# Moving the down weights' requests from SyncE's queue to ScalarE's, in a hybrid S5 / attention encoder with a mixture of experts

## The chip, the core and the metric

The kernel runs on one core of a Trainium2 chip. The metric is device time of that core in microseconds (us). Weights come from device memory (HBM) into SBUF by the core's 16 DMA engines. A transfer is asked for by an instruction on the queue of an engine: SyncE (SP), ScalarE (ACT) or GpSimd (POOL). The trace shows such an instruction as SPq, ACTq or POOLq and the transfers that follow as packets of queue q1 (asked for by SyncE), q10 (by ScalarE) and q0 (by GpSimd).

## The reference

Two layers over 256 tokens of width 1024 in float32. Layer 0 mixes tokens with a bidirectional S5 scan, layer 1 with neighbourhood attention. After each comes a mixture of 32 experts of which each token uses two, then a gated input embedding ("ple"). The part that matters here:

```python
for g in range(N_GROUPS):                       # 4 groups of 8 experts
    a = jnp.einsum('td,edf->tef', t, w_gate[g]) # 1024 -> 256
    u = jnp.einsum('td,edf->tef', t, w_up[g])   # 1024 -> 256
    act = jax.nn.silu(a) * u * combine[:, g, :, None]
    y = y + jnp.einsum('tef,efd->td', act, w_down[g])   # 256 -> 1024
```

Each expert has three weight matrices of 1 MB: gate, up and down. All 32 experts of both layers are loaded, 96 MB a layer.

## The kernel before

The tokens are sorted by expert (gather, line 1765) and the experts are worked through in 16 pairs a layer. For pair p TensorE does `gate_up(p)` (line 1794, 32 matmuls), then, one pair behind, the transposes of the activations of pair p-1 (line 1806), two pairs behind the combination `combine(p-2)` (line 1835), and `down(p-1)` (line 1825, 16 matmuls). So the program of TensorE is gate_up(p), act_T(p-1), combine(p-2), down(p-1), gate_up(p+1), and so on. ScalarE does `silu(p)` (line 847) when gate_up(p) is done, and `out_hi(p-1)` (line 855), two evictions of the outputs of down(p-1), the second when down(p-1) is done (semaphore `d_done`). VectorE takes those further (line 1317).

The weights lie in six ring slots, one for each expert, so for three pairs at a time. A slot has a part for gate and up, and a part for down, and each part is asked for again when its last reader is done. The first three pairs of a layer are asked for in full before the layer's experts begin. After that SyncE's program is: gate and up of pair p once gate_up(p-3) is done (four transfers of 1 MB, `load_gate_up`, lines 437 and 438), then the downs of pair p-1 once down(p-4) is done (two transfers of 1 MB, `load_down`, line 446), then pair p+1. At the end of a layer stand the two downs of pair 14 and the two of pair 15. Then come the weights of the ple stage (line 426). PE waits for gate and up of a pair on one semaphore of the slot (`loaded`), for down on another (`down_loaded`).

Of the kernel before, what the change touches and what calls it, by code (L numbers as in the profile page):

```python
# [48 lines left out]
NP = NE // 2  # L49
# [13 lines left out]
def program(nc, I, out):  # L63
    ctx = ExitStack()
    with ctx:
        sems = {}

        def S(name):
            if name not in sems:
                sems[name] = ctx.enter_context(nc.semaphore(name))  # L70
            return sems[name]
# [4 lines left out]
        def at(name, shape, dtype, off):  # L76
            return nc.alloc_sbuf_tensor_at(name, shape, dtype, offset=off)
# [70 lines left out]
        ring = [at(f"ring{s}", [P, RS], F32, A_R + s * RS * 4) for s in range(4)]  # L148
# [10 lines left out]
        items = []  # L159
# [9 lines left out]
        moe_item = []  # L169
# [26 lines left out]
        prev, nth, last, cnt = [], [], {}, {}  # L196
        for n, (s, _) in enumerate(items):
            prev.append(last.get(s))
            last[s] = n
            cnt[s] = cnt.get(s, 0) + 1  # L200
            nth.append(cnt[s])
# [4 lines left out]
        done = {IT["w_in"]: ("u_done", 1)}  # L206
# [9 lines left out]
        down_loaded = [S(f"down_loaded{s}") for s in range(6)]  # L216
# [160 lines left out]
        def overflow(eng, i, body, first=None, last=None):  # L377


            eng.wait_ge(S("many_ready"), i + 1)  # L380
            with eng.If(eng.value_load(many[0:1, 0:1], min_val=0, max_val=2 * T) > 0):
                if first:
                    first()
                with eng.Fori(0, NOV) as n:
                    body(n)
                if last:
                    last()
# [24 lines left out]
        def _(sp):  # L412
            def load(n):
                s, parts = items[n]
                if prev[n] is not None:
                    name, value = done[prev[n]]
                    sp.wait_ge(S(name), value)
                for j, (c, src) in enumerate(parts):
                    w = 1
                    for m in src.shape[1:]:  # L420
                        w *= m
                    dst = ring[s][:, c:c + w]
                    if len(src.shape) == 3:
                        dst = dst.rearrange("p (k n) -> p k n", k=src.shape[1])

                    sp.dma_start(dst, src).then_inc(loaded[s], 48 - 16 * (len(parts) - 1) if j == 0 else 16)

            def load_gate_up(n, first):

                s, (gate_, up_, down_) = items[n]  # L430
                if not first:
                    i, e = (0, n - moe_item[0]) if n < moe_item[1] else (1, n - moe_item[1])
                    sp.wait_ge(S("gu_done"), NP * i + e // 2 - 2)
                elif prev[n] is not None:
                    name, value = done[prev[n]]
                    sp.wait_ge(S(name), value)
                sp.dma_start(ring[s][:, 0:2048], gate_[1]).then_inc(loaded[s], 32)
                sp.dma_start(ring[s][:, 2048:4096], up_[1]).then_inc(loaded[s], 16)

            def load_down(n, first):  # L440

                s, (gate_, up_, down_) = items[n]
                if not first:
                    name, value = done[prev[n]]
                    sp.wait_ge(S(name), value)
                sp.dma_start(ring[s][:, 4096:6144], down_[1]).then_inc(down_loaded[s], 16)

            sp.dma_start(lam[:, 0], I["s5_lam_re"][0].rearrange("d g p -> g d p")).then_inc(S("lam_loaded"), 16)
# [34 lines left out]
            for i in range(2):  # L483
                m0 = moe_item[i]
                for e in range(6):
                    if items[m0 + e][0] == 4:
                        if i == 0:
                            sp.wait_ge(S("x_ready"), 1)
                        else:
                            sp.wait_ge(S("pv_done"), NH)  # L490
                    load_gate_up(m0 + e, True)
                    load_down(m0 + e, True)
                for p in range(3, NP + 1):
                    if p < NP:
                        load_gate_up(m0 + 2 * p, False)
                        load_gate_up(m0 + 2 * p + 1, False)
                    if p >= 4:
                        load_down(m0 + 2 * p - 2, False)
                        load_down(m0 + 2 * p - 1, False)
                wviews = [I["moe_w_gate"][i].rearrange("g j (p k) n -> p (g j) (k n)", k=KD),  # L500
                          I["moe_w_up"][i].rearrange("g j (p k) n -> p (g j) (k n)", k=KD),
                          I["moe_w_down"][i].rearrange("g j (p k) n -> p (g j) (k n)", k=2)]

                def more(n):
                    sp.wait_ge(S(f"ov_free{i}"), n + 1)
                    e = n % NE
                    for c, w in enumerate(wviews):
                        sp.dma_start(ring[S_OV][:, 2048 * c:2048 * c + 2048],
                                     w[:, bass.ds(e, 1), :].rearrange("p e n -> p (e n)"))\
                            .then_inc(S(f"ov_loaded{i}"), 16)  # L510

                for n in (IT["ple"][i][1], IT["ple"][i][0], IT["ple"][i][2]):
                    load(n)
                if i == 0:
                    load(IT["qkv"][0])
                sp.wait_ge(S("d_done"), 2 * NP * (i + 1))
                overflow(sp, i, more, lambda: sp.sem_inc(S(f"ov_free{i}"), 1),
                         lambda: sp.wait_ge(S(f"ov_free{i}"), NOV + 1))
                if i == 0:
                    for n in IT["qkv"][1:] + IT["wo"]:  # L520
                        load(n)
# [170 lines left out]
        def _(ac):  # L692
# [117 lines left out]
            def square(i, t):  # L810
                ac.wait_ge(x_part[i], 2 * t + 2)
                ac.activation(hsq[:, t, :], x[:, t, :], ACT.Square, accum_out=fss[:, t:t + 1]).then_inc(S("fss_ready"), 1)

            def x_evict(i, t):
                ac.wait_ge(S("x_T"), 2 * (TT * i + t) + 1)
                ac.activation(hT[:, 0:4, P * t:P * t + P], PS[:, 2 * t, :].rearrange("p (k t) -> p k t", k=4),
                              ACT.Copy).then_inc(S("xT_a"), 1)

            def token_split(i, t):

                ac.wait_ge(S("frstd_ready"), TT * i + t + 1)
                link(ac.activation(hf[:, t], x[:, t, :].rearrange("p (a k) -> p k a", k=KD), ACT.Copy,
                                   scale=frstd[:, t:t + 1]))
                ac.activation(hhi[:, t], hf[:, t], ACT.Copy).then_inc(S("hhi_ready"), 1)
# [13 lines left out]
            def gather_evict(i, k):  # L838
                ac.wait_ge(S("gather_done"), KD * i + k + 1)
                ac.activation(xg[:, k, :], PS[:, GBANK[k], :], ACT.Copy, scale=gT[:, i, k:k + 1])\  # L840
                    .then_inc(S("xg_ready"), 1)
# [8 lines left out]
            def out_hi(i, p):  # L850
                for n in range(2):
                    ac.wait_ge(S("d_done"), 2 * (NP * i + p) + n + 1)
                    if n == 0 and NP * i + p:
                        ac.wait_ge(S("comb_done"), NP * i + p)
                    ac.activation(ohi[:, 512 * n:512 * n + 512], PS[:, 2 + n, :], ACT.Copy)\  # L855
                        .then_inc(S("ohi_ready"), 1)

            def moe(i):
                square(i, 1)
                x_evict(i, 1)  # L860
                token_split(i, 1)
                ac.wait_ge(S("top_ready"), i + 1)
                for t in range(TT):
                    ac.activation(gex[:, t, :], lg[:, t, NE:NE + NG], ACT.Exp, bias=ngm[:, t:t + 1],
                                  accum_out=gsum[:, t:t + 1])
                ac.activation(e21[:, :], dlt[:, :], ACT.Exp).then_inc(S("gex_ready"), 1)
                ac.wait_ge(S("gT_loaded"), 80)
                for k in range(KD):
                    gather_evict(i, k)
                for p in range(NP):  # L870
                    silu(i, p)
                    if p:
                        out_hi(i, p - 1)
                out_hi(i, NP - 1)
                ac.wait_ge(S("p_T"), i + 1)
                ac.activation(pT[:, :, :].rearrange("p k t -> p (k t)"), PS[:, 0, :], ACT.Copy).then_inc(S("pT_ready"), 1)
                moe_more(i)
# [1160 lines left out]
```

## Time and profile before

| | us |
|---|---|
| median of 3 runs | 876.13 |
| lowest to highest | 876.1 to 878.23 |
| the profiled execution | 876.75 |
| its span in the trace | 875.0 |
| PE busy | 776.4 (89%) |
| ACT busy | 237.9 (27%) |
| data moved | 245.46 MB |

The span is the time from the first to the last instruction in the trace; the execution's own time is 1.75 us more. Where a page has 40 slices, each is 21.9 us. The experts of layer 0 run from 183 to 403 us, those of layer 1 from 623 to 843 us.

### The profile page before, as it was taken

Reading aid. Unit: us, or ns where it says so; the run is one execution under the profiler, and the core shown is the slowest. Engines: PE = TensorE matmul, PEld = TensorE weight load, DVE = VectorE, ACT = ScalarE, POOL = GpSimd, SP = SyncE. Lnnn points to the kernel's source line nnn. Section 1 sums busy time; section 2 is a strip of 40 time slices with the busy share of each in tenths; the row PEclk is TensorE's granted clock in tenths of the full one; section 3 lists DMA queues with packets and bytes.
Section 4 is the critical chain, followed back from the end, with each engine's and each line's share of the span. In section 5 each row is a group of like instructions: output and inputs, shape, how many; then the busy total and the mean of one; then the engine's idle time right before and its main releaser. Section 6 shows DMA issues by size and latency. Waiting matters only on the chain.

```text
span 875.0 us, 10464 instructions
## 1 busy us (share of the span) xinstructions
PE 776.4 (89%) x3995; PEld 425.9 (49%) x3995; DVE 395.4 (45%) x720; ACT 237.9 (27%) x422; POOL 191.0 (22%) x198
## 2 busy tenths in 40 slices
PE   2667879599999998999999878996999999998997
PEld 1556734543433333346878654545533343333456
DVE  6996742623232322136668658515322232222264
ACT  3323123331111101016575444422310111100153
POOL 5874500221110110000056364002211011010000
PEclk9988979699999999999999959996999999999999
DMA  6035070979999999996787660175199999999761
GB/s 217 1 56 194 5 289 1 390 281 425 421 421 420 421 421 419 422 411 218 260 209 248 250 194 1 54 300 223 57 422 421 420 421 422 421 420 421 321 253 48
DMA packets 61091, 245.46 MB, mean 281 GB/s; under 512 B 19667, under 2 KB 20721, under 8 KB 36081
## 3 DMA queue, kind: packets, MB, share of 16 engines
q1 hardware_dynamic: 56752, 240.36, 69.1%
q0 software_dynamic: 1600, 4.26, 2.1%
q8 instruction: 33, 0.54, 0.3%
q10 hardware_dynamic: 2688, 0.17, 0.2%
q14 instruction: 18, 0.14, 0.0%
HBM read 243.16 MB, written 1.60 MB: 280 GB/s over the span
## 4 chain that ended last, share of the span: by engine, by line
PE 83%; DVE 7%; issue 5%; ACT 2%; POOL 2%; DMA 1%; SPq 0%; ACTq 0%; DVEq 0%; POOLq 0%
PE PS L1794 26%; PE PS L1825 13%; PE PS L1545 10%; PE PS L1835 7%; PE PS L1727 3%; PE PS L2008 3%; PE PS L1765 2%; PE PS L1669 2%; PE PS L1967 2%; PE PS L1988 2%; PE PS L1603 2%; PE PS L1915 2%; PE PS L1806 1%; PE PS L1684 1%; POOL qrs L685 1%
## 5 line engine op out<-in xcount | busy, mean ns | idle before, releaser
L1794 PE MATMUL PS<-ring,xe 128*64 128x512 f32 x1024 | 231.0, 604 | 15.9 <-issue 13.5
L1794 PEld LDWEIGHTS PS<-ring,xe 128*64 128x64 f32 x1024 | 79.8, 139 | 163.7 <-issue 163.7
L1825 PE MATMUL PS<-ring,actT 128*64 128x512 f32 x512 | 116.9, 598 | 1.7 <-DVE actT L1303 1.4
L612 POOL COPY xe<-xg 128x512 f32 x60 | 47.1, 786 | 300.1 <-PE PS L1794 297.7
L1317 DVE TENSOR_TENSOR olo<-PS,ohi 128x512 fp32r<-128x512 f32 x64 | 44.3, 692 | 123.5 <-ACT ohi L855 123.5
L1303 DVE COPY actT<-PS 128x256 f32<-128x256 f32 x32 | 13.6, 425 | 175.6 <-PE PS L1806 175.6
L855 ACT ACTIVATE ohi<-PS 128x512 fp32r<-128x512 f32 x64 | 38.3, 598 | 153.0 <-PE PS L1825 153.0
L1008 DVE SCALAR_TENSOR_TENSOR ringr<-ring,gT,dwh 128x512 fp32r<-128x512 f32 x80 | 62.9, 838 | 26.7 <-ACT dwh L726 25.4
L847 ACT ACTIVATE act<-PS 128x256 f32<-128x256 f32 x32 | 12.3, 385 | 225.5 <-PE PS L1794 225.5
L1825 PEld LDWEIGHTS PS<-ring,actT 128*64 128x64 f32 x512 | 34.7, 136 | 67.1 <-issue 67.1
L1545 PE MATMUL PS<-ringr,rawh 128*128 128x512 f32 x160 | 63.4, 396 | 0.8 <-DVE ringr L1008 0.8
L1545 PE MATMUL PS<-dwh,rawh 128*128 128x512 f32 x160 | 62.3, 389 | 0.0
L1545 PE MATMUL PS<-dwh,rawl 128*128 128x512 f32 x160 | 62.3, 389 | 0.0
L726 ACT ACTIVATE dwh<-ring,gT 128x512 fp32r<-128x512 f32 x80 | 52.7, 719 | 34.4 <-PE PS L1545 29.8
L1835 PE MATMUL PS<-ohi,selT 128*128 128x512 f32 x128 | 53.4, 418 | 0.3
L1835 PE MATMUL PS<-olo,selT 128*128 128x512 f32 x128 | 50.2, 392 | 0.0
L1727 PE MATMUL PS<-ring,yT 128*128 128x512 f32 x64 | 32.1, 659 | 5.1 <-DVE yT L1173 5.1
L1545 PEld LDWEIGHTS PS<-ringr,rawh 128*128 128x128 f32 x160 | 30.0, 188 | 7.9 <-issue 1.9
L579 POOL TENSOR_TENSOR rstd<-ms,mhalf 128x2 f32<-128x2 f32 x4 | 2.9, 718 | 140.4 <-DVE ms L990 137.1
L1545 PEld LDWEIGHTS PS<-dwh,rawl 128*128 128x128 f32 x160 | 30.1, 188 | 6.5 <-issue 0.5
L1545 PEld LDWEIGHTS PS<-dwh,rawh 128*128 128x128 f32 x160 | 30.0, 188 | 6.4
L2008 PE MATMUL PS<-ring,oT 128*128 128x512 f32 x64 | 27.9, 594 | 0.5 <-DVE oT L1489 0.5
(323 smaller groups left out, 1031.3 us busy)
## 6 DMA issues: line engine op xcount, KB each, us to landing
ring<-in_moe_w_gate SPq DMA_DIRECT2D x64, 1024.0 KB
ring<-in_moe_w_up SPq DMA_DIRECT2D x64, 1024.0 KB
ring<-in_moe_w_down SPq DMA_DIRECT2D x64, 1024.0 KB, 24.2
ring<-in_nat_w_qkv SPq DMA_DIRECT2D x6, 2048.0 KB
ring<-in_ple_w_gate SPq DMA_DIRECT2D x4, 2048.0 KB
ring<-in_s_w_out SPq DMA_DIRECT2D x2, 2048.0 KB
ring<-in_nat_w_o SPq DMA_DIRECT2D x2, 2048.0 KB
ring<-in_s_w_in SPq DMA_DIRECT2D x1, 2048.0 KB
```

The source lines that it names most:

```text
L612: pool.tensor_copy(xe[:, e % 4, :, :], xg[:, :, bass.ds(first, CAP)]).then_inc(S("xe_ready"), 1)
L726: ins = ac.activation(dwh[:, c, k], dense_w(n, c)[0][:, k], ACT.Copy, scale=gT[:, g, 2 * c + k:2 * c + k + 1])
L855: ac.activation(ohi[:, 512 * n:512 * n + 512], PS[:, 2 + n, :], ACT.Copy)\
L1008: ins = stt(lo[:, k], w[:, k], gT[:, g, 2 * c + k:2 * c + k + 1], dwh[:, c, k].bitcast(F32), ALU.mult, ALU.subtract)
L1317: tt(olo[:, cs], PS[:, 2 + n, :], ohi[:, cs].bitcast(F32), ALU.subtract)\
L1545: ins = mm(PS[:, b0 + t, :], a_[:, 2 * c + k, r], b_, start=(c, k, w) == (0, 0, 0), stop=(c, k, w) == (3, 1, 2))
L1603: ins = mm(PS[:, 4 + a // 2, T * (a % 2):T * (a % 2) + T], w_in[:, k, P * a:P * a + P], s5hT[:, k, :], start=k == 0, stop=k == KD - 1)
L1727: ins = mm(PS[:, 4 + 2 * (n % 2) + w, :], yT[4][:, k, P * t:P * t + P], wv[:, k, 512 * c:512 * c + 512], start=k == 0, stop=k == 3)
L1794: ins = mm(PS[CAP * h_:CAP * h_ + CAP, 0, :].rearrange("p (u f) -> p u f", u=2), xe[:, (2 * p + h_) % 4, k, :], wv[h_][:, k], start=k == 0 ...
L1825: ins = mm(PS[CAP * h_:CAP * h_ + CAP, 2 + n, :], actT[:, k, CAP * h_:CAP * h_ + CAP], wd[h_][:, k, 512 * n:512 * n + 512], start=k == 0, ...
L1835: ins = mm(PS[:, 4 + 2 * n + t, :], selT[:, p % 2, P * t:P * t + P], o_half[:, 512 * n:512 * n + 512], start=(p, w) == (0, 0), stop=(p, w) ...
L2008: ins = mm(PS[:, 6 + n % 2, :], oT[:, k, P * t:P * t + P], wv[:, k, :], start=k == 0, stop=k == KD - 1)
```

## The change

The downs of pairs 3 to 15 of each layer, 52 transfers of 1 MB in all, are asked for by ScalarE instead of SyncE. ScalarE asks for those of pair p+2 behind silu(p) and out_hi(p-1), with the same wait as before (down(p-1) done), which out_hi(p-1) has already had. Gate and up of all pairs, and the downs of pairs 0 to 2, stay with SyncE. Semaphores, buffers and everything else are as before.

```diff
-                for p in range(3, NP + 1):
-                    if p < NP:
-                        load_gate_up(m0 + 2 * p, False)
-                        load_gate_up(m0 + 2 * p + 1, False)
-                    if p >= 4:
-                        load_down(m0 + 2 * p - 2, False)
-                        load_down(m0 + 2 * p - 1, False)
+                for p in range(3, NP):
+                    load_gate_up(m0 + 2 * p, False)
+                    load_gate_up(m0 + 2 * p + 1, False)
...
+            def load_down(n):
+
+                s, (gate_, up_, down_) = items[n]
+                name, value = done[prev[n]]
+                ac.wait_ge(S(name), value)
+                ac.dma_start(ring[s][:, 4096:6144], down_[1]).then_inc(down_loaded[s], 16)
...
                     silu(i, p)
                     if p:
                         out_hi(i, p - 1)
+                        if p + 2 < NP:
+                            load_down(moe_item[i] + 2 * p + 4)
+                            load_down(moe_item[i] + 2 * p + 5)
```

SyncE's program in layer 0, from gate and up of pair 3 on (ring_96 to ring_101 are the six slots), before:

```order
42 L437 DMA ring_98<-in_moe_w_gate 128x2048
43 L438 DMA ring_98<-in_moe_w_up 128x2048
44 L437 DMA ring_99<-in_moe_w_gate 128x2048
45 L438 DMA ring_99<-in_moe_w_up 128x2048
46 L437 DMA ring_96<-in_moe_w_gate 128x2048
47 L438 DMA ring_96<-in_moe_w_up 128x2048
48 L437 DMA ring_97<-in_moe_w_gate 128x2048
49 L438 DMA ring_97<-in_moe_w_up 128x2048
50 L446 DMA ring_98<-in_moe_w_down 128x2048
51 L446 DMA ring_99<-in_moe_w_down 128x2048
52 L437 DMA ring_100<-in_moe_w_gate 128x2048
53 L438 DMA ring_100<-in_moe_w_up 128x2048
```

The same place with the change:

```order
46 L437 DMA ring_96<-in_moe_w_gate 128x2048
47 L438 DMA ring_96<-in_moe_w_up 128x2048
48 L437 DMA ring_97<-in_moe_w_gate 128x2048
49 L438 DMA ring_97<-in_moe_w_up 128x2048
50 L437 DMA ring_100<-in_moe_w_gate 128x2048
51 L438 DMA ring_100<-in_moe_w_up 128x2048
```

The two downs between gate and up of pair 4 and of pair 5 are gone from here, and so at every later pair. ScalarE's program at the beginning of the experts of layer 0 (xg is the gathered input, act the activation, ohi the output's eviction), before:

```order
46 L840 ACTIVATE xg<-PS,gT 128x512 x8
47 L847 ACT_TABLE_LOAD
48 L847 ACTIVATE act<-PS 128x256 x2
49 L855 ACTIVATE ohi<-PS 128x512 x2
50 L847 ACTIVATE act<-PS 128x256
51 L855 ACTIVATE ohi<-PS 128x512 x2
```

The same place with the change:

```order
48 L840 ACTIVATE act<-PS 128x256 x2
49 L848 ACTIVATE ohi<-PS 128x512 x2
50 L856 DMA ring_98<-in_moe_w_down 128x2048
51 L856 DMA ring_99<-in_moe_w_down 128x2048
52 L840 ACTIVATE act<-PS 128x256
53 L848 ACTIVATE ohi<-PS 128x512 x2
54 L856 DMA ring_96<-in_moe_w_down 128x2048
55 L856 DMA ring_97<-in_moe_w_down 128x2048
```

Two requests now stand between each pair of evictions and the next silu.

## Rows read from the trace of the kernel before

**Rows 1.** The page's slices of 21.9 us: DMA share in tenths, and GB/s
```profile
DMA  6035070979999999996787660175199999999761
GB/s 217 1 56 194 5 289 1 390 281 425 421 421 420 421 421 419 422 411 218 260 209 248 250 194 1 54 300 223 57 422 421 420 421 422 421 420 421 321 253 48
```

**Rows 2.** Chain that ended last, layer 0: start us, us, what
```profile
291.98 6.87 PE PS L1794 x32
...
301.07 3.58 PE PS L1825 x16
304.65 6.87 PE PS L1794 x32
...
317.33 1.02 issue
318.34 7.09 PE PS L1794 x32
...
331.23 2.04 issue
333.27 7.09 PE PS L1794 x32
...
361.06 2.02 issue
363.08 8.78 PE PS L1794 x32
...
377.67 0.32 issue
377.99 7.09 PE PS L1794 x32
...
393.62 3.65 PE PS L1825 x16
```

**Rows 3.** The same chain, layer 1
```profile
744.21 6.87 PE PS L1794 x32
...
756.88 1.17 issue
758.04 7.09 PE PS L1794 x32
...
817.95 7.09 PE PS L1794 x32
```

**Rows 4.** DMA, 190.5 to 387.5 us: mean, packets and MB by queue, requests
```profile
DMA packets 11302, 82.42 MB, mean 418 GB/s; under 512 B 1248, under 2 KB 1248, under 8 KB 1248
...
q1 hardware_dynamic: 11292, 82.29, 100.7%
...
ring<-in_moe_w_gate SPq DMA_DIRECT2D x26, 1024.0 KB
ring<-in_moe_w_up SPq DMA_DIRECT2D x26, 1024.0 KB
ring<-in_moe_w_down SPq DMA_DIRECT2D x26, 1024.0 KB, 26.1
```

**Rows 5.** DMA, 240 to 380 us
```profile
DMA packets 8086, 58.93 MB, mean 421 GB/s; under 512 B 898, under 2 KB 898, under 8 KB 898
```

**Rows 6.** Timeline of SyncE's queue: start us, us, line, request
```profile
190.31 0.35 SPq L437 DMA_DIRECT2D ring<-in_moe_w_gate  x1
...
203.30 0.80 SPq L446 DMA_DIRECT2D ring<-in_moe_w_down  x2
...
292.02 7.24 SPq L446 DMA_DIRECT2D ring<-in_moe_w_down  x2
...
350.43 12.84 SPq L446 DMA_DIRECT2D ring<-in_moe_w_down  x4
377.71 0.33 SPq L426 DMA_DIRECT2D ring<-in_ple_w_proj  x1
```

**Rows 7.** DMA, 450 to 460 us: requests of GpSimd (q0) and SyncE (q1) together
```profile
q0 software_dynamic: 470, 1.29, 63.8%
q1 hardware_dynamic: 474, 0.97, 41.6%
```

**Rows 8.** Timeline of ScalarE, 435 us, first request of ScalarE in the program
```profile
435.62 0.58 ACTq L928 DMA_DIRECT2D qkw<-in_nat_q_norm  x1
```

**Rows 9.** DMA, 435.6 to 437.6 us: packets, requests with us to landing
```profile
DMA packets 400, 0.82 MB, mean 410 GB/s; under 512 B 0, under 2 KB 0, under 8 KB 400
...
q1 hardware_dynamic: 400, 0.82, 105.0%
...
qkw<-in_nat_q_norm ACTq DMA_DIRECT2D x2, 0.2 KB, 4.1
```

**Rows 10.** Timeline of ScalarE, one pair of layer 0
```profile
292.03 0.60 ACT L855 ACTIVATE ohi<-PS 128x512 fp32r<-128x512 f32 x1 [1.12 <-PE PS L1825]
298.89 0.38 ACT L847 ACTIVATE act<-PS 128x256 f32<-128x256 f32 x1 [6.27 <-PE PS L1794]
```

**Rows 11.** Line 446 in full: ns min/median/max, and us to landing
```profile
L446 SPq DMA_DIRECT2D ring<-in_moe_w_down x64: 327/481/6296, 113.6 to 801.2; - x64
...
DMA to landing us min/median/max: 8.8/24.2/30.0
```

**Rows 12.** Stretches within gate_up(14): us, busy by engine, granted clock, DMA, GB/s
```profile
363.10:367.40 4.30, 4.30 (x13) 1.57 (x15) 0.11 (x1) 0.00 (x0) 0.00 (x0) 0.60 1.01 419
367.40:371.90 4.50, 4.50 (x23) 1.64 (x20) 0.00 (x0) 0.00 (x0) 0.00 (x0) 1.00 1.02 422
```

More of the change, by code:

```diff
@@ L438, in load_gate_up @@
                 sp.dma_start(ring[s][:, 2048:4096], up_[1]).then_inc(loaded[s], 16)
-            def load_down(n, first):
+            def load_down(n):
                 s, (gate_, up_, down_) = items[n]
-                if not first:
-                    name, value = done[prev[n]]
-                    sp.wait_ge(S(name), value)
                 sp.dma_start(ring[s][:, 4096:6144], down_[1]).then_inc(down_loaded[s], 16)
@@ L491, in _ @@
                     load_gate_up(m0 + e, True)
-                    load_down(m0 + e, True)
-                for p in range(3, NP + 1):
-                    if p < NP:
-                        load_gate_up(m0 + 2 * p, False)
-                        load_gate_up(m0 + 2 * p + 1, False)
-                    if p >= 4:
-                        load_down(m0 + 2 * p - 2, False)
-                        load_down(m0 + 2 * p - 1, False)
+                    load_down(m0 + e)
+                for p in range(3, NP):
+                    load_gate_up(m0 + 2 * p, False)
+                    load_gate_up(m0 + 2 * p + 1, False)
                 wviews = [I["moe_w_gate"][i].rearrange("g j (p k) n -> p (g j) (k n)", k=KD),
@@ L856, in out_hi, with load_down @@
                         .then_inc(S("ohi_ready"), 1)
+            def load_down(n):
+                s, (gate_, up_, down_) = items[n]
+                name, value = done[prev[n]]
+                ac.wait_ge(S(name), value)
+                ac.dma_start(ring[s][:, 4096:6144], down_[1]).then_inc(down_loaded[s], 16)
             def moe(i):
```

## The prediction, made before the changed kernel ran

> **What bounds the kernel now.** I began with the slices of the page [rows 1]. In both stretches of experts the DMA share is 9 tenths or more and the rate stands at 419 to 425 GB/s, slice after slice but the last of each: the weights are loaded at a rate that doesn't rise. Next I read the chain that ended last, in order of time [rows 2]. Up to pair 10 one gate_up follows the other without a wait: 304.65 - 291.98 = 12.67 us for a pair. From pair 11 on (318.34) there is a wait of 1 to 2 us ahead of gate_up ("issue": TensorE waits for nothing that the profile names, which here is a landing), and the period is 333.27 - 318.34 = 14.93 us. That is what six transfers of 1 MB take: 6 x 1.0486 MB / 421 GB/s [rows 5] = 14.94 us, or 2.49 us each. So the experts start with three pairs in store, lose 2.26 us of that lead with each pair, and are bound by DMA from pair 11 to pair 15. Layer 1 repeats it, with the first wait at 758.04 instead [rows 3].
>
> The last gate and up of layer 0 let gate_up(15) begin at 377.99. The position of a transfer in the line tells when it lands. Line: gate and up of pairs 3 to 15 are 13 x 4 = 52 transfers, the downs of the same pairs 26, 78 in all (26 of each kind in [rows 4]). The first is asked for at 190.31 [rows 6], and the queue never runs dry until the last (mean 418 GB/s over the whole stretch, 421 once under way). SyncE's program puts the four downs of pairs 14 and 15 at the end (the row with x4 in [rows 6]), so the last "up" is number 74. 190.31 + 74 x 2.49 = 374.6, and gate_up(15) starts 3.4 us later; the same working for pair 11 (number 50: 314.8) gives 3.5 us against 318.34. I take 3.4 us as start-up and landing. Number 78 is served at 384.5, while the last down starts only at 393.62 [rows 2]. Downs therefore have time to spare at the end, and gate and up have none. **What decides this change is whether gate and up keep their places in the line.**
>
> **The change, part by part.**
>
> *SyncE loses 26 requests a layer.* It spends up to 7.24 us on two of them and 12.84 us on the last four [rows 6], against 0.80 us at the beginning: when some ten transfers are outstanding, a request has to wait for a place. Being rid of that is worth nothing by itself, since the DMA engines are busy all the same [rows 5], and a request accepted earlier is not served earlier at the same rate. The ple weights at 377.71 wait for down(13), not for the queue. Gain 0.
>
> *ScalarE gains 26 requests a layer.* The semaphore wait costs nothing, out_hi has had it. The issue costs about 0.8 us for two (at 203.30 in [rows 6]). They go into the idle time between the second eviction and the next silu, 6.27 us [rows 10]. If ScalarE's requests must wait for a place as SyncE's do, 7.24 us for two would delay silu by 1 us. Silu(p+1) is wanted by gate_up(p+2), which comes after transposes, combine and down, 12.67 - 6.87 = 5.8 us after gate_up(p+1) ends; silu and VectorE's product take about 1 us of them. So cost 0 up to roughly 6.27 + 4.8 = 11 us of blocking, and from there one for one.
>
> *The downs are asked for at the same point of the work*, 0.6 us later (the second eviction). Nothing comes of it alone: they land a median 24.2 us after the request [rows 11].
>
> *The downs are in a line of their own.* This is the term that counts. Where requests of two engines are pending together, the trace has one long stretch: 450 to 460 us, GpSimd's bias loads (q0) beside SyncE's (q1). In it q0 moved 470 packets and q1 474 [rows 7]: the DMA engines take turns, packet for packet. Both kinds of MoE transfer are 1 MB in rows of the same size, so turns by packet, or by request, are equal shares of the rate while both lines have work. The Trainium skill ("DMA: Bandwidth & Descriptors", section Queues, rings and completion order) says that each DMA engine goes round the queues it has work for, packet by packet; the trace agrees (470 to 474), and by the rule the sum is the one below.
>
> With equal shares the two downs of a pair need at most 4 x 2.49 = 9.95 us from request to last byte, instead of 24.2. There is a request of two every 12.7 to 15 us, so the downs are always served soon, and whatever backlog there is falls on gate and up alone. At the end: the last downs (pair 15) are asked for once down(12) is done, a wait of about 2 us and a period of 14.93 before gate_up(15) starts, so some 16.5 us before; less the 3.4 of landing and the 0.6 of ScalarE 12.5 us remain, and they need 9.95. So all 26 downs are served before the last "up", which goes from number 74 to number 78: 4 x 2.49 = +9.95 us, gate_up(15) at 387.9. A second way: a gate_up now has up to four more downs ahead of it. Pair 7 has number 20 + 6 and would get 30, 190.3 + 74.7 + 3.4 = 268.4; without a wait it would start at 291.98 - 2 x 12.67 = 266.64. So the waits start at pair 7 rather than 11, and 268.4 + 8 x 14.93 = 387.8. The two agree.
>
> Nothing behind gate_up(15) gives it back: act_T, combine, down(14) and down(15) follow in a row as they do now, the ple weights wait on down(13) and down(15), and these have moved by the same 9.95 us. The first pairs of layer 1 are asked for after the attention stage, as before. Layer 1 has the same line and the same waits. **Sum: 2 x 9.95 = +19.9 us.** On the profiled execution (span 875.0, time 876.75) that is a span of 894.9; on the median, 876.13, it is 896.0.
>
> *The clock.* After a 2.02 us wait gate_up(14) took 8.78 us in place of 7.09, with a granted clock of 0.60 in its first half and 1.00 in the second [rows 2, 12]. While DMA is the bound this hides in the next wait. If it falls on gate_up(15), where it doesn't now, it costs 1.7 us a layer: 0 to +3.4, I take 0 (of five gate_ups behind a wait in layer 0 one shows it).
>
> **The rivals.**
>
> 1. *One common line, in order of arrival, with contended places.* For: at 435.62 ScalarE asks for a few bytes [rows 8] while one request of SyncE is in work. In the next 2 us the DMA engines move 400 packets of q1 and not one of q10, and it lands after 4.1 us [rows 9]. So ScalarE's request wasn't slipped in among q1's packets as GpSimd's were; making the descriptors may be common to both queues. Against: it had a single request in front of it, so it can't tell a common line from turns by whole requests, and the latter gives the shares above. In a common line with some ten places both engines wait for one, and the downs overtake one or two of the four transfers of gate and up that SyncE still holds: the last "up" goes to number 75 or 76, +2.5 to +5.0 us a layer, 881.1 to 886.1. Chance 0.20.
>
> 2. *Same order as now, no difference.* The common line without overtaking: 876.1, within 2.6. The Trainium skill (same page, section Issuing engines are not separate DMA queues) says that requests from several engines end on the same 16 DMA engines and save only sequencer time, "usually small relative to the DMA itself"; read as "no effect" it gives 876.1. [Rows 5] agree that there is no rate to gain. Chance 0.12.
>
> 3. *Faster, by gate and up going first.* If ScalarE's line got much less than its share, gate and up would run ahead and the downs come last. Number 78 lands at 384.5 + 3.4 = 387.9, the last down now starts at 393.62, so at most 5.7 us a layer, 864.7. It decides if the downs are still in time for each pair; against it is the equal count of [rows 7]. Chance 0.07.
>
> 4. *ScalarE held up beyond its 11 us.* Four requests cost SyncE 12.84 us [rows 6]. If two did that to ScalarE in the nine pairs bound by DMA, 1.8 us each, part of it in TensorE's wait: up to 2 x 9 x 1.8 = 32 us on top, above 900. Against: its line holds at most four or so requests. Chance 0.05.
>
> **How the numbers follow.** Equal shares has 0.56, with its range 893 to 899.4 (with the clock's 3.4 above and a few us below, if the last down isn't quite finished before the last "up"). A measurement of this kernel can tell about 0.3%, 2.6 us. Slower by more than that: 0.56 + 0.05 + most of rival 1 (0.17) = 0.78. Within: 0.12 + 0.03 = 0.15. Faster: 0.07. The range 876 to 900 holds the first case, rival 1 and half of rival 2.
>
> **What would show it.** In the changed trace: the first "issue" of 1 us or more ahead of a gate_up near 268 us (pair 7) rather than 317 (pair 11), and gate_up(15) near 388 in layer 0 and near 817.95 + 19.9 = 837.9 in layer 1; downs landing about 10 us after an ACTq request rather than 24; SyncE's requests for gate and up at about 0.4 us each throughout, as fewer are outstanding; 421 GB/s as before. A common line would show ScalarE's requests at 2 us or more each and landings over 20 us. The forecast is wrong if gate_up(15) of layer 0 begins before 384.

## The result, and the profile of the changed kernel

| | us |
|---|---|
| before, median of 4 runs | 876.12 |
| changed, median of 4 runs (894.98 to 899.08) | 897.79 |
| ratio | 1.0237, 95% interval 1.0208 to 1.0266 |
| changed, the profiled execution | 897.75, span 896.0 |

The change makes the kernel 2.4% slower. The forecast was 896.0, slower with a chance of 0.78.

On the page of the changed kernel, the slices (21.9 us before, 22.4 us now) answer to [rows 1]. The rate in the stretches of experts is the same, 418 to 423 GB/s in the slices that lie wholly in them, and there is a queue q10 of 54.70 MB, nearly all of it the 52 downs:

```profile
DMA  6044061979999999965787650373499999999361
GB/s 212 1 72 172 6 282 45 424 285 418 423 420 421 421 422 421 421 253 189 262 204 263 257 149 1 114 315 135 163 420 421 421 422 421 421 421 421 128 248 47
...
q1 hardware_dynamic: 49264, 185.83, 52.8%
q10 hardware_dynamic: 10176, 54.70, 14.8%
```

The chain that ended last in layer 0 (start us, us, what), which answers to [rows 2]; TensorE's gate_up is line 1797 now:

```profile
266.23 2.56 issue
268.79 7.09 PE PS L1797 x32
...
281.68 1.98 issue
283.66 8.79 PE PS L1797 x32
...
387.63 0.24 issue
387.87 7.09 PE PS L1797 x32
```

The wait ahead of gate_up begins at pair 7 (268.79) where it began at pair 11 (318.34), and gate_up(15) starts at 387.87 instead of 377.99. From gate_up(0), 182.88 us here and 183.25 before, it is 205.0 us instead of 194.7. The same chain in layer 1, which answers to [rows 3]:

```profile
835.21 2.04 issue
837.25 8.78 PE PS L1797 x32
```

Here gate_up(15) comes at 837.25 instead of 817.95, and its first half falls into the lower clock: 8.78 us for 7.09, with a granted clock of 0.61 in its first 4.4 us and 1.00 behind.

The DMA view from 240 to 380 us answers to [rows 5]: mean rate 421 GB/s as before, now from two queues. The second fence is the request's own line (count, ns min/median/max) and its landing, which answers to [rows 11]:

```profile
DMA packets 8099, 58.95 MB, mean 421 GB/s; under 512 B 909, under 2 KB 909, under 8 KB 909
...
q1 hardware_dynamic: 5290, 38.50, 66.1%
q10 hardware_dynamic: 2800, 20.33, 35.0%
```

```profile
L856 ACTq DMA_DIRECT2D ring<-in_moe_w_down x52: 334/413/1192, 202.9 to 820.7; - x52
...
DMA to landing us min/median/max: 8.9/12.0/15.2
```

A down lands 12.0 us after its request in place of 24.2. That is the whole "gain" of the change, and nobody waited for it. Within 4 us in which both lines have work (270 to 274), the DMA view shows who was served:

```profile
q10 hardware_dynamic: 108, 0.88, 53.0%
q1 hardware_dynamic: 112, 0.79, 47.9%
```

108 packets to 112: turns packet for packet. Over the 10 us from 269.5 on it is 275 to 290, and 2.08 to 2.11 MB. This is cleaner evidence than [rows 7]. In the stretch of [rows 7] 156 of the 944 packets are under 512 B. SyncE's 0.97 MB are just 474 rows of 2 KB, so the tiny ones are GpSimd's, and its 470 are about 314 rows of data and 156 tiny packets. The 470 to 474 is a turn each only if a tiny packet counts as a turn.

The DMA view of the end of layer 0, 384.3 to 387 us, shows who was served last:

```profile
q1 hardware_dynamic: 108, 0.75, 66.7%
q10 hardware_dynamic: 14, 0.02, 2.4%
```

ScalarE's last two downs are all but through at 384.3, SyncE's gates and ups run on, almost alone, to 387, and gate_up(15) starts at 387.87. All 26 downs were served ahead of the last "up".

### The profile page after: what moved, and what is told of

It reads as the page before. It is cut to its first block, busy times and chain, and to the rows that moved or that the text cites. A ratio compares the mean times of both kernels' runs of the same rounds, so it can differ in the third digit from the quotient of the medians.

```text
span 896.0 us, 10464 instructions
## 1 busy us (share of the span) xinstructions
PE 782.7 (87%) x3995; PEld 430.4 (48%) x3995; DVE 395.3 (44%) x720; ACT 237.9 (27%) x422; POOL 191.2 (21%) x198
## 3 DMA queue, kind: packets, MB, share of 16 engines
q10 hardware_dynamic: 10176, 54.70, 14.8%
## 4 chain that ended last, share of the span: by engine, by line
PE 82%; DVE 7%; issue 6%; ACT 2%; POOL 2%; DMA 1%; SPq 0%; ACTq 0%; DVEq 0%; POOLq 0%
PE PS L1797 26%; PE PS L1828 13%; PE PS L1548 10%; PE PS L1838 6%; PE PS L2011 3%; PE PS L1730 3%; PE PS L1768 2%; PE PS L1672 2%; PE PS L1970 2%; PE PS L1991 2%; PE PS L1606 2%; PE PS L1918 2%; PE PS L1687 1%; PE PS L1809 1%; POOL qrs L678 1%
## 5 line engine op out<-in xcount | busy, mean ns | idle before, releaser
L1797 PE MATMUL PS<-ring,xe 128*64 128x512 f32 x1024 | 236.5, 616 | 30.6 <-issue 28.3
L1797 PEld LDWEIGHTS PS<-ring,xe 128*64 128x64 f32 x1024 | 84.3, 141 | 180.8 <-issue 180.8
```

Of the source, the lines that this page charges most:

```text
L1797: ins = mm(PS[CAP * h_:CAP * h_ + CAP, 0, :].rearrange("p (u f) -> p u f", u=2), xe[:, (2 * p + h_) % 4, k, :], wv[h_][:, k], start=k == 0 ...
```

## The experiments

The theory: the DMA engines work through a line of 78 transfers of 2.49 us a layer; the two queues take equal turns; a pair can start when the transfers ahead of its last "up" are served, and the change lets downs that nobody needs yet pass gates and ups that TensorE waits for. The rivals: a second queue, or ScalarE's time for its requests, costs by itself; each moved request costs its part; or the loss has one common source outside the layers. Each ratio below is against runs of the kernel before that were taken beside the experiment (medians 876.24 to 876.83 us).

**e8_last_four: only the last downs moved.** ScalarE asks for the downs of pairs 14 and 15 (eight of 52 transfers); the others stay in SyncE's program where they were.

```diff
-                        if p + 2 < NP:
+                        if NP - 4 <= p < NP - 2:
...
+                    if 4 <= p < NP - 1:
+                        for n in (m0 + 2 * p - 2, m0 + 2 * p - 1):
+                            ...
+                            load_down(n)
```

> One part of the change alone: only the downs of pairs 14 and 15 (eight of the 52 transfers) are asked for by ScalarE, those of pairs 3 to 13 by SyncE in the order of the kernel before. Theory (what counts is that these four a layer overtake the last gates and ups): the last up is number 78 as in the full change, gate_up(15) some 205 us behind gate_up(0) instead of 194.8, and the time is that of the full change, 895 to 898, though only eight requests are moved and the waits begin no earlier than pair 12 or 13. Rival (each request moved costs its part): 8/52 of 21.7 us, 879.6.

Measured: 897.49 us (ratio 1.0233, 1.0208 to 1.0258), the time of the full change. The waits ahead of gate_up(11) to (13) are those of the kernel before (1.1 and twice 2.0 us); the large one is ahead of gate_up(14):

```profile
361.42 8.17 issue
369.60 8.40 PE PS L1803 x32
...
383.80 2.56 issue
386.36 8.55 PE PS L1803 x32
```

Gate_up(14) is 187.9 us behind gate_up(0) (181.71) where it was 179.8, so between three and four places were lost at once. Gate_up(15) is 204.7 us behind, as in the full change (205.0). Eight requests do the damage of 52. This run strikes out "each request costs its part" and "ScalarE's time for requests": 44 requests fewer on ScalarE changed nothing.

**e9_not_last: all but the last downs moved.** The downs of pairs 3 to 13 from ScalarE, the last four of each layer from SyncE, behind everything.

```diff
-                        if p + 2 < NP:
+                        if p < NP - 4:
...
+                    if p >= NP - 1:
+                        for n in (m0 + 2 * p - 2, m0 + 2 * p - 1):
+                            ...
+                            load_down(n)
```

> The other part alone: the downs of pairs 3 to 13 (44 transfers) are asked for by ScalarE, those of pairs 14 and 15 by SyncE behind all gates and ups, as in the kernel before. Theory, in the form that the run with ups on ScalarE taught (each pair has its own place in the line, and the end is the latest over the pairs of its landing plus TensorE's 12.67 us for each pair behind it): the last up is number 74 again, but pair 13 has number 66 in place of 62 and starts at 358.0, so gate_up(15) at 358.0 + 2 x 12.67 = 383.4, up to 385 with the lower clock: 5.4 to 7 us a layer, 887 to 890. By the place of the last up alone: 876. By requests moved: 44/52 of 21.7 us, 894.6.

Measured: 885.29 us (ratio 1.0091, 1.0068 to 1.0115). The chain in layer 0:

```profile
357.77 0.30 issue
358.08 7.09 PE PS L1803 x32
...
370.97 6.87 PE PS L1803 x32
...
383.64 6.87 PE PS L1803 x32
```

Pair 13 starts at 358.08 (expected 358.0), the last two follow without a wait, and gate_up(15) starts at 383.64 (expected 383.4). The time is 2 us under the expected 887, and the profile shows where. From the start of gate_up(0) to the end of gate_up(15) the layers are 5.5 and 5.2 us longer than before, about as expected, but the stretch between them, from the end of gate_up(15) of layer 0 to gate_up(0) of layer 1, took 235.7 us where the kernel before has 237.8. That stretch, with the attention stage in it, has neither the line nor the change, and its granted clock differs from profile to profile: 0.93 over the stretch here, 0.92 in the kernel before and in the changed one (237.6 us), 0.90 in e1, which is the longest of all profiles (241.1 us). The parts also don't add up (e8 +21, e9 +8.5, both +21.7), and they need not: the end is the latest over the pairs, not a sum.

**e1_lag: ScalarE asks one pair later.**

```diff
-                        if p + 2 < NP:
-                            load_down(moe_item[i] + 2 * p + 4)
-                            load_down(moe_item[i] + 2 * p + 5)
+                        if 2 <= p and p + 1 < NP:
+                            load_down(moe_item[i] + 2 * p + 2)
+                            load_down(moe_item[i] + 2 * p + 3)
```

> The changed kernel with ScalarE's two requests moved one pair later: behind out_hi(p-1) it asks for the downs of pair p+1 instead of pair p+2. Nothing else differs. My theory (equal turns of the two lines, so that what counts is how many downs are served ahead of the last up): the downs of pair 15 are now asked for only when gate_up(15) can start, so the last up is number 76 of 78 in place of 78. Each layer ends 2 x 2.49 = 5.0 us later than in the kernel before, not 10: 876.1 + 10.0 = 886.1, gate_up(15) of layer 0 near 382.9, waits from about pair 9 on. Rival A (a second line costs by itself, by switching between queues or by ScalarE's time for requests): as many requests as in the change, so about 897.8. Rival B (the downs are what arrives late): asking for them later makes it slower than 897.8.

Measured: 889.31 us (ratio 1.0121, 1.0083 to 1.0159); 886.1 was expected. The chain in layer 0:

```profile
291.03 2.21 issue
293.23 7.09 PE PS L1797 x32
...
380.53 1.96 issue
382.50 8.78 PE PS L1797 x32
```

The first wait is at pair 9 and gate_up(15) at 382.50, both as expected (382.9): two places in the line are worth 5 us a layer, half of four (5.4 us in layer 0, 5.2 in layer 1, against the kernel before). The 3 us more than expected come mostly not from the line. In the profiled execution (891.36 us, the slowest of four from 885.58 on) 1.7 us are the lower clock, which fell on gate_up(15) of layer 0, and 3.3 us lie in the stretch between the layers, 241.1 us at a granted clock of 0.90 (see e9). The other three executions weren't profiled. As many requests from ScalarE as in the change, so a cost of the second queue by itself is out as the main cause, and late downs are too.

**e2_layer0: the change in layer 0 only.** `if i == 0 and p + 2 < NP` on ScalarE, and the downs of layer 1 back in SyncE's program.

> The change in layer 0 alone; in layer 1 SyncE asks for the downs as in the kernel before. Theory: each layer pays for itself, 9.95 us a layer and 1.7 us where the lower clock falls on gate_up(15). Layer 0 showed 9.9 us at gate_up(15) in the changed kernel and no slow gate_up(15), so 876.1 + 10 = 886.1, and the other 11 us belong to layer 1. Rival (one part of the loss is common, for instance at the change of layers or in the attention stage): well away from half, under 883 or over 890.

Measured: 887.15 us (ratio 1.0113, 1.0089 to 1.0137), half of the loss. Gate_up(15) is 204.7 us behind gate_up(0) in layer 0 and 194.9 in layer 1. Each layer pays for itself.

**e3_ups: the up weights go with the downs.** ScalarE asks for up and down, SyncE for gate only.

```diff
+                    if p + 3 < NP:
+                        load_up(moe_item[i] + 2 * p + 6)
+                        load_up(moe_item[i] + 2 * p + 7)
                     if p:
                         out_hi(i, p - 1)
```

> The changed kernel, and the up weights of pairs 3 to 15 too are asked for by ScalarE (behind silu(p), for pair p+3), so ScalarE makes four requests a pair and SyncE two (gate). Theory: gate runs ahead in its own line, and in ScalarE's line up and down keep the order of the kernel before. In front of the last up stand 26 gates, 25 ups and 22 downs: it is number 74 again, as before. So 876 us, gate_up(15) of layer 0 near 378, with two lines in use and twice the requests on ScalarE. Rival A (two lines, or requests on ScalarE, cost by themselves): 898 or more. Rival B (the line that has fewer bytes always wins and something else lags): between.

Measured: 881.44 us (ratio 1.0049, 1.0029 to 1.0069), so neither the 876 expected nor the 898 of the rival. With twice as many requests from ScalarE as the change has, three quarters of the loss is gone. What stays is an error in my counting. The chain in layer 0:

```profile
351.58 3.04 issue
354.63 8.78 PE PS L1808 x32
...
369.22 6.87 PE PS L1808 x32
...
381.88 6.87 PE PS L1808 x32
```

The last "up" is in time: gate_up(14) and (15) start without a wait. But gates of pairs 14 and 15, alone in SyncE's line, ran ahead of the ups of pair 13, which starts at 354.63 instead of 348.2. The DMA view from 346 to 349 us has 165 packets of q10 and 23 of q1: SyncE's line had run empty, with the gates of pair 14 served while ups of pair 13 were still to come. (The trace names no landing of a single transfer, so that it was these ups is worked out, not read.) From there TensorE needs 12.67 us a pair and once the lower clock. I had counted the place of the last "up" only. Each pair has its own place, and a later start of pair 13 can't be caught up once the store is empty. The expectation for e9 was worked out in this form, and its starts came true within 0.3 us.

**e4_rows4k: the downs in packets of 4 KB.**

```diff
-                ac.dma_start(ring[s][:, 4096:6144], down_[1]).then_inc(down_loaded[s], 16)
+                for k in range(2):
+                    ac.dma_start(ring[s][:, 4096 + 1024 * k:5120 + 1024 * k], down_[1][:, 1024 * k:1024 * k + 1024])\
+                        .then_inc(down_loaded[s], 16)
```

> The changed kernel with each of ScalarE's 52 downs asked for as two requests of half the columns, so in packets of 4 KB while gate and up stay at 8 KB. Theory (turns are taken packet by packet, whatever a packet's size): the downs get 4 KB for each 8 KB of gate and up, a third of the rate in place of half, which is just their share of the bytes. Two downs need 15 us where they needed 10, so they run ahead of the last up by hardly more than in the kernel before: worked out pair by pair with a third, the layer ends 2.8 us later than before, 876.1 + 5.5 = 881.6. If turns were shared out by bytes: 897.8 as in the change.

Measured: 889.05 us (ratio 1.0124, 1.0097 to 1.0151); 881.6 was expected for turns by packet, 897.8 for turns by bytes. DMA from 240 to 380 us:

```profile
DMA packets 10664, 58.31 MB, mean 416 GB/s; under 512 B 1184, under 2 KB 1184, under 8 KB 5920
...
q1 hardware_dynamic: 5327, 38.79, 66.6%
q10 hardware_dynamic: 5328, 19.40, 34.8%
```

Over these 140 us the two lines have equal packet counts and a byte ratio of 2 to 1, which fits turns by packet but is also what the program asks for, so by itself it proves little. The waits begin at pair 9 (293.0) rather than 7, so the downs did run ahead less. But the rate fell from 421 to 416 GB/s, which on 78 transfers is 2.3 us a layer; with the expected 2.8 that makes 5.1, and gate_up(15) of layer 0 came 200.2 us behind gate_up(0), 5.4 more than before. The lower clock fell on it as well:

```profile
381.30 2.19 issue
383.49 8.78 PE PS L1799 x32
```

So my term for the order fits, though it is not measured apart from the rate, and I had left out what smaller packets cost in rate.

**e5_halfreq: the downs in requests of 64 partitions.**

```diff
-                ac.dma_start(ring[s][:, 4096:6144], down_[1]).then_inc(down_loaded[s], 16)
+                for k in range(2):
+                    ac.dma_start(ring[s][64 * k:64 * k + 64, 4096:6144], down_[1][64 * k:64 * k + 64, :])\
+                        .then_inc(down_loaded[s], 16)
```

> The changed kernel with each of ScalarE's 52 downs asked for as two requests of 64 partitions each, in packets of 8 KB as in the change. Twice the requests on ScalarE, half the size, same packets. Theory (turns by packet): nothing changes, 897.8 within 3 us. Rival (turns by whole request): the downs get a third of the rate, 881.6 as forecast for the run with 4 KB packets. Rival (ScalarE's time for requests is part of the loss): slower than the change, by 0.8 us a pair where TensorE waits, so up to 910.

Measured: 1094.94 us (ratio 1.2505, 1.2454 to 1.2556), which nothing had expected. DMA from 245 to 255 us:

```profile
DMA packets 364, 2.48 MB, mean 248 GB/s; under 512 B 61, under 2 KB 61, under 8 KB 61
...
q1 hardware_dynamic: 187, 1.29, 55.0%
q10 hardware_dynamic: 177, 1.19, 48.4%
```

While such requests are in work, the rate of both lines together is 248 GB/s instead of 421. As a time the run says nothing on the theory. Its packets do: 177 to 187 with both lines pending, though ScalarE's requests are half as large. Turns by whole request would have given one to two. So a turn is shorter than a request, though this is seen at 248 GB/s. In the changed kernel, at 421 GB/s, each half microsecond from 270 to 274 us has 9 to 18 packets of either line, which fits turns by packet.

**e6_early: the line starts earlier, in halves.** The kernel before, with gate and up of pair 3 asked for in halves of 4 KB rows, the first ones when half of gate_up(0) is done.

```diff
+                for c0 in (0, 1024):
+                    sp.wait_ge(...)
+                    for n in (moe_item[i] + 6, moe_item[i] + 7):
+                        ...
+                            sp.dma_start(ring[s][:, c + c0:c + c0 + 1024], src[:, c0:c0 + 1024])\
```

> Not the change but the kernel before, with one edit meant to move the start of the line: gate and up of pair 3 are asked for in halves, the first halves (rows k 0 to 3, four requests of 0.5 MB) when the first half of gate_up(0) is done, the rest when gate_up(0) is done as before. Theory (from pair 11 on a layer ends by the position of the last up in an unbroken line of 2.49 us a piece, counted from its first request): the line starts some 3.5 us earlier, when the DMA engines stand idle, and everything counted from it is earlier by as much: 876.1 - 2 x 3.5 = 869.1, gate_up(15) of layer 0 near 374.5. Rival (the waits before gate_up are not a matter of the line, but for instance of landing or of the clock): 876.1.

Measured: 876.33 us (ratio 0.9989, 0.9972 to 1.0007): no gain. The requests did begin 3.4 us earlier, in the timeline of SyncE's queue:

```profile
186.58 0.33 SPq L449 DMA_DIRECT2D ring<-in_moe_w_gate  x1
...
190.01 0.33 SPq L449 DMA_DIRECT2D ring<-in_moe_w_gate  x1
```

But the rate broke in while the halves were served. DMA from 191 to 195 us:

```profile
DMA packets 269, 1.00 MB, mean 251 GB/s; under 512 B 24, under 2 KB 24, under 8 KB 269
```

By 200 us the DMA engines had moved 4.03 MB since 186 us against 3.43 in the kernel before, 1.4 us of work ahead where 3.4 were meant. SyncE asks for pair 4 only from 198.26 on, when pair 3 is almost through, and the rate was 369 and 348 GB/s from 200 to 202. From 220 to 370 us the lead is 0.4 MB, 1 us, and 0.3 us of that is the whole program's earlier start. Gate_up(11) starts at 318.16, only 0.2 us earlier than before, and where the rest of the lead went is open. Why 4 KB halves ran at 251 GB/s here and at nearly full rate in e4 is open. The run neither confirms nor refutes the theory, since it changed the rate together with the start.

**e7_prefetch: one transfer taken out of the line.** The kernel before, with the down weights of pair 3's first expert loaded into the place of `hlo` while the DMA engines stand idle.

```diff
+        early = at("early", [P, 2048], F32, A_H + 8192)
...
+                s, (gate_, up_, down_) = items[m0 + 6]
+                sp.wait_ge(S("gather_done"), KD * (i + 1))
+                sp.wait_ge(down_loaded[s], 16 * (nth_moe[m0 + 6] - 1))
+                sp.dma_start(early[:, :], down_[1]).then_inc(down_loaded[s], 16)
...
-                    wd.append(ring[items[it][0]][:, 4096:6144].rearrange("p (k n) -> p k n", k=2))
+                    w_ = early[:, :] if 2 * p + h_ == 6 else ring[items[it][0]][:, 4096:6144]
+                    wd.append(w_.rearrange("p (k n) -> p k n", k=2))
```

> Not the change: the kernel before with one transfer of each layer taken out of the line. The down weights of pair 3's first expert are loaded into a place of their own (the place of hlo, free once the gather is done), asked for by SyncE at the end of the gather, so that they move while the DMA engines would stand idle ahead of the first request of the line. Theory (a layer ends by the place of the last up in an unbroken line of 2.49 us a piece): the line has 77 pieces, the last up is number 73, both layers end 2.49 us earlier: 876.3 - 5.0 = 871.3, gate_up(15) of layer 0 at 192.3 us behind gate_up(0) where it is 194.8 in the kernel before. Rival (the run with halved first requests, which gained nothing, shows that an earlier start isn't worth anything because something else sets the end): 876.3.

Measured: 869.7 us (ratio 0.9914, 0.9895 to 0.9933), faster than both kernels. SyncE's queue and the chain in layer 0:

```profile
181.19 0.33 SPq L497 DMA_DIRECT2D early<-in_moe_w_down  x1
189.94 0.35 SPq L438 DMA_DIRECT2D ring<-in_moe_w_gate  x1
```

```profile
329.63 0.82 issue
330.45 7.09 PE PS L1800 x32
...
373.15 2.00 issue
375.15 7.09 PE PS L1800 x32
```

Gate_up(15) is 192.3 us behind gate_up(0), to the tenth what was expected, and 192.7 in layer 1 (195.1 before). A place in the line is worth its 2.5 us in both directions. The layers give 4.9 us; the median moved by 7.1, the profiled span by 6.1. Of the 1.2 us beyond in the profile, 0.4 lie ahead of layer 0 and 0.9 between the layers, where the granted clock was 0.94 for 0.92; the rest of what the median gained has no cause that these runs show.

## Why the prediction was right

- **What bounds the kernel.** A line of transfers of 2.49 us, unbroken from its first request: confirmed by the same 421 GB/s with two queues, by e7 (one transfer less, 2.5 us less a layer) and by e2 (each layer by itself). "Unbroken from its first request" is too much: nothing moves for the first 0.9 us behind the request at 190.31 (DMA view of the kernel before), and full rate begins only near 192.3. The 3.4 us of the prediction held this and the landing in one term, taken from the same trace.
- **The term that counts.** "The last up goes from number 74 to number 78": gate_up(15) was forecast for 387.9 and came at 387.87; the first wait for 268.4 and came at 268.79. e8 shows it as the cause, not only the size: moving just the four transfers a layer that do the passing gives the full loss. The two layers of the changed profile are 10.3 and 9.6 us longer, together the 19.9 of the sum.
- **Equal turns by packet.** [Rows 7] had it from GpSimd's and SyncE's queues, with the tiny packets counted. The changed kernel has 108 to 112 for ScalarE's and SyncE's, and e5 keeps the count nearly equal with requests of half the size. Here the Trainium skill ("DMA: Bandwidth & Descriptors", section Queues, rings and completion order), which says that the DMA engines go round their queues by packet, agrees with the trace in the turns. Its figure for a packet, typically some 9 to 17 descriptors, isn't what was counted here: the packets of these rows are 8 KB, one row of a transfer, and by e5 a turn is shorter than a request of 64 rows, on average four for each of the 16 engines.
- **Landing of the downs.** About 10 us forecast, 12.0 in the median. I had left out the start: in the 3 us behind the request at 266.29 the DMA view shows q10 with hardly a packet:

```profile
q1 hardware_dynamic: 165, 1.21, 96.9%
q10 hardware_dynamic: 23, 0.06, 4.9%
```

  ScalarE's request begins only after some 3 us while SyncE's line has work. The same holds for the requests at 281.74 and 371.08, whose first packets come near 285.0 and 374.4. From its start on a pair of downs takes the 10 us that were forecast (269.5 to 279.5). That the sum stood is in part luck: two errors cancel in its margin. It gave the last downs 12.5 us, of which they need 9.95. In fact they waited 3.3 us first, but from the end of the line to gate_up(15) there was about 1 us and not 3.4, so they were through at 384.3, some 2.6 us ahead of the last "up". The late start is the delay that [rows 8, 9] show, and on which rival 1 was built. So that rival had a true observation and drew too much from it: the delay is a start-up of each request, not a common line.
- **SyncE's relief and ScalarE's load.** Both forecast at 0. SyncE's requests for gate fell from a median of 457 to 362 ns, without effect (a few for up still took 2 to 2.8 us). ScalarE's took 413 ns each (0.82 us for two), and the next silu began as before, with 6.27 us idle ahead of it in the stretch without waits. ScalarE's queue isn't held up, so rival 4 is out.
- **The clock.** Taken at 0 and bounded at 1.7 us a layer. In the profiled execution it fell on gate_up(15) of layer 1 (8.78 us, granted clock 0.61 and then 1.00). That is the difference between the forecast span of 894.9 and 896.0, less 0.6 us elsewhere. The four runs of the changed kernel lie between 894.98 and 899.08. None, one or two such cases a run would spread them so, but so would the stretch between the layers, which was 3.3 us longer in e1. Only one execution was profiled, so this stays open.
- **Rivals 2 and 3.** Not the same time and not faster: the downs had no reason to be late or early, and what mattered was whom they passed. The Trainium skill (same page, section Issuing engines are not separate DMA queues) says that a second issuing engine saves only time on the sequencer, and the trace agrees that it gains no rate, 421 GB/s with one and with two. Read as "no effect", as rival 2 read it, it is 21.7 us off here, because the order of service changes.

## What to carry to other kernels

When DMA is the bound, a queue is also an order of service, and moving the less urgent transfers to a second queue gives them half of the rate while the urgent ones wait; ask of each transfer who needs it when, and leave what is needed last in the same line, behind the rest. Count places: the end of such a stretch is the latest, over all consumers, of (transfers served ahead of it) x (time of one) plus the work behind it, and it isn't enough to count the last one (e3, e9). What pays is a transfer moved out of the busy line into a time in which the DMA engines stand idle, as in e7.

## What was not expected of the hardware

- Requests of 64 partitions brought the whole DMA rate from 421 to 248 GB/s while they were in work, for the other queue's transfers too (e5: 1094.94 us). Rows of the same 8 KB over 128 partitions don't do that (421 GB/s in the changed kernel). The cause wasn't tried.
- Halves of rows (4 KB) cost 1% of the rate in e4 (from 421 to 416 GB/s), but for 4 us after the idle time in e6 they ran at 251 GB/s. Left open.
- A request on ScalarE's queue began 3.2 to 3.4 us after it was issued while SyncE's queue had work (three requests looked at), though from then on it took every second packet. With nothing else in work the first packets of SyncE's request at 190.31 came 0.9 us behind it, and the full rate 2 us behind it.
- The stretch between the layers, which no edit of these runs touched, took from 235.7 to 241.1 us in the profiles, and its granted clock goes with it: 0.93 to 0.94 where it took 235.7 to 236.9 us, 0.92 where it took 237.6 to 237.9, 0.90 where it took 241.1. That spread is as large as the effect of two places in the line, so a difference of 2 or 3 us between two profiled executions says little until it is placed in a stretch.
